# Layer 0's expert table: 80 slots per expert instead of 96

## The reference, cut to what matters

```python
expert = grp[:, None] * EXPERTS_PER_GROUP + local      # two experts per token
counts = jnp.bincount(e_flat, length=N_EXPERTS)
def expert_block(args):
    xb, e = args
    hmid = jax.nn.silu(xb @ e_gate[e]) * (xb @ e_up[e])
    return hmid @ e_down[e]
```

## Time and profile before

| what | value |
|---|---|
| runs | 2742.33, 2744.23, 2746.5 us |
| profiled execution, its own time | 2742.03 us |
| its span | 2740.4 us |
| mean granted TensorE clock | 0.959 of full |
| TensorE busy | 2502.4 us (91%) |
| VectorE busy | 1038.0 us (38%) |
| ScalarE busy | 491.3 us (18%) |
| GpSimd busy | 231.8 us (8%) |
| layer 0's experts in the trace | about 1009 to 1561 us from the span's start |
| layer 1's experts in the trace | about 2215 to 2710 us |

### The profile page before, as it was taken

How to read it: one execution, slowest core, us unless ns; L and a number is a source line. 1 busy time by engine, 2 the same in 40 slices (tenths; PEclk the granted TensorE clock), 3 DMA queues, 4 the chain that set the end, 5 groups by cost and what they waited for, 6 DMA issues and landing times.

```text
span 2740.4 us, 45413 instructions
## 1 busy us (share of the span) xinstructions
PE 2502.4 (91%) x19000; PEld 1530.5 (56%) x19001; DVE 1038.0 (38%) x2398; ACT 491.3 (18%) x978; POOL 231.8 (8%) x391
## 2 busy tenths in 40 slices
PE   7999999999998969999999999999999878888874
PEld 3455545454443457777777655667676544444442
DVE  2226536256465342222222251636457432111112
ACT  2023222222222011111111021323222111101110
POOL 3000001000000001111111110000000011111111
PEclk9989999999999979999999999999999979999997
DMA  9111118242324359999999762123465769999994
GB/s 293 61 62 62 47 43 305 114 142 85 112 87 131 125 193 370 370 374 381 378 383 387 292 203 92 62 77 104 145 185 179 257 265 409 410 418 413 415 404 169
DMA packets 153139, 616.72 MB, mean 225 GB/s; under 512 B 17121, under 2 KB 21489, under 8 KB 136465
## 3 DMA queue, kind: packets, MB, share of 16 engines
q1 hardware_dynamic: 126850, 557.88, 54.4%
q0 software_dynamic: 26192, 57.51, 6.5%
HBM read 598.37 MB, written 46.31 MB: 235 GB/s over the span
## 4 chain that ended last, share of the span: by engine, by line
PE 71%; DMA 15%; DVE 9%; issue 2%; ACT 2%; POOL 0%; DVEq 0%; SPq 0%; POOLq 0%; ACTq 0%
DMA ring<-in_e_down_dram 14%; PE bank L1660 13%; PE bank L1396 12%; PE bank L1288 11%; PE bank L1278 7%; PE score_banks L1677 4%; PE bank L1409 4%; PE score_banks L1697 3%; PE score_banks L1682 2%; PE bank L1567 2%; PE score_banks L1445 2%; PE turned_banks L1455 2%; PE bank L1643 1%; PE bank L1469 1%; PE bank L1317 1%
## 5 line engine op out<-in xcount | busy, mean ns | idle before, releaser
L1660 PEld LDWEIGHTS bank<-scr,ring 128*64 128x64 f32 x8192 | 340.6, 137 | 14.2 <-issue 14.2
L1396 PE MATMUL bank<-HT,ring 128*128 128x512 f32 (+1 forms) x1024 | 347.4, 494 | 0.8 <-ACT scr L1004 0.4
L1660 PE MATMUL bank<-scr,ring 128*64 128x96 f32 x8192 | 346.7, 247 | 1.2 <-DVE scr L2382 1.2
L1288 PE MATMUL bank<-ring,HT 128*128 128x512 f32 (+1 forms) x800 | 303.0, 535 | 0.0
L1653 PE MATMUL bank<-ring,scr 128*64 128x256 f32 x2048 | 239.8, 388 | 44.5 <-DMA ring<-in_e_gate_dram 22.8
L1396 PEld LDWEIGHTS bank<-HT,ring 128*128 128x128 f32 x1024 | 192.1, 192 | 143.2 <-issue 130.9
L1288 PEld LDWEIGHTS bank<-ring,HT 128*128 128x128 f32 x800 | 151.6, 193 | 142.3 <-issue 136.3
L1653 PEld LDWEIGHTS bank<-ring,scr 128*64 128x64 f32 x2048 | 146.5, 139 | 141.4 <-DMA ring<-in_e_gate_dram 41.5
L1278 PE MATMUL bank<-HT,ring 128*128 128x512 f32 (+1 forms) x512 | 196.1, 542 | 1.8 <-ACT HT L1004 1.8
L1697 PE MATMUL score_banks<-ring,scr 128*64 128x512 f32 x512 | 133.7, 670 | 35.5 <-DMA ring<-in_e_down_dram 33.8
L1278 PEld LDWEIGHTS bank<-HT,ring 128*128 128x128 f32 x512 | 97.0, 192 | 91.9 <-issue 88.4
(11 more groups left out here) (267 smaller groups left out, 2715.7 us busy)
## 6 DMA issues: line engine op xcount, KB each, us to landing
ring<-in_e_up_dram SPq DMA_DIRECT2D x64, 2048.0 KB, 22.0
ring<-in_e_down_dram SPq DMA_DIRECT2D x64, 2048.0 KB, 20.9
ring<-in_e_gate_dram SPq DMA_DIRECT2D x64, 2048.0 KB, 21.2
ring<-in_w_in_dram SPq DMA_DIRECT2D x34, 2048.0 KB, 8.0
ring<-in_w_mod_dram SPq DMA_DIRECT2D x32, 1024.0 KB, 5.2
ring<-in_w_mod_dram SPq DMA_DIRECT2D x8, 2048.0 KB, 19.5
ys<-consts POOLq DMA_DIRECT2D x1, 12288.0 KB, 41.7
ring<-in_w_branch_dram SPq DMA_DIRECT2D x4, 2048.0 KB, 7.9
```

What stands on the lines that cost most here:

```text
L1288: m = pe.matmul(bank[:, 0:width], HT[:, k, t * P:t * P + P], w[:, k, 0:width], start=k == 0, stop=k == KT_D - 1)
L1396: m = pe.matmul(bank[:, 0:NQ], w[:, k, (ft % 4) * P:(ft % 4) * P + P], HT[:, k, 0:NQ], start=k == 0, stop=k == KT_D - 1)
L1660: m = pe.matmul(ps[bank][rows_, f * cap:f * cap + cap], w[:, k, f * P + hf * HALF:f * P + hf * HALF + HALF], XTv[:, k, :], start=k == 0, s ...
```

## The change

The table of layer 0 holds 80 slots per expert. The count of column groups stays; the second part of the down product has 16 slots (64 to 79) instead of 32. All that is sized by CAP[0] follows: the transposed tokens, the streamed width in `hidden` (96 to 80), the width of the silu and of the product (384 to 320 elements), the slots of the two indirect DMAs, the blocks of the general path (6 to 7) and the part of `ys` that is cleared early (12288 to 10240 KB). An expert with more than 80 tokens in layer 0 would take the general path, instead of one with more than 96.

```diff
-CAP = (96, 64)
+CAP = (80, 64)
@@ down_held
-                            m = pe.matmul(ps[5][t * 32:t * 32 + 32, 0:256], hv[:, f, HALF:cap], w[:, f, t * 256:t * 256 + 256],
+                            m = pe.matmul(ps[5][t * 32:t * 32 + cap - HALF, 0:256], hv[:, f, HALF:cap], w[:, f, t * 256:t * 256 + 256],
                                           start=f == 0, stop=f == 3)
@@ expert, on VectorE
-                        last = dve.tensor_copy(YS[HALF:cap, j, t * 256:t * 256 + 256], ps[5][t * 32:t * 32 + 32, 0:256])
+                        last = dve.tensor_copy(YS[HALF:cap, j, t * 256:t * 256 + 256], ps[5][t * 32:t * 32 + cap - HALF, 0:256])
```

## The result

The changed kernel took 2714.96 us, median of 4 runs (2712.81 to 2717.82), against 2745.36 us for the kernel before, median of 4 (2742.33 to 2749.89). The ratio is 0.9887, with a 95% interval of 0.9872 to 0.9903. The profiled execution took 2716.85 us, of which the span is 2715.1. Against the profiled execution of before it is 25 us shorter, while the medians are 30 us apart. The profiled execution of before lies 3.4 us under its median, and that of after 1.9 us over.

A forecast was written before the change was run, and what follows sets the result against it. TensorE paces layer 0's experts at 17.22 us, loads close behind at 17.76; layer 1 waits for weights. Loads at 17.0 end the loop 31.2 us sooner, less 1 for clock: 30 off 2742.0 is 2712, median 2714; range 2690 to 2738.

The forecast's parts named there:

- Part 1: Streamed width in the hidden part of layer 0's experts (L1660): 1.7 us less per expert, bounds 0 and 1.8.
- Part 2: Second part of the down product, 16 loaded columns instead of 32: 0 taken, between none and 0.3 us.
- Part 3: Before layer 0's expert loop: slot matmuls 0.5 us and first gate product 1.2 less; first gate load at about 1014.5.
- Part 4: Layer 0's weight loads become late and set the end: 17.0 us per expert, ends 15.95 and 17.76.
- The depth: Weight ring's lead in layer 0, 16.5 us, lasts about 11 experts; the other 19 wait for loads.
- stands whatever TensorE does: Claim that layer 0's loads before the change take 17.73 us per expert independent of TensorE, the DMA queue never being empty.
- The 1 us for the lower clock: Taken off the 31.2 us gain for stretches where TensorE, waiting 1.5 us per expert, falls to the lower clock.
- the unchanged pace: Rival 1: layer 0's loads keep their pace since the tokens don't change; 8.4 us gained, 2736; chance 0.18.
- the loads keep up: Rival 2: layer 0's loads take 15.95 us or less, TensorE sets the end; 2689 to 2692; chance 0.12.
- The uneven dealing: Rival 3: 80-slot indirect DMAs weigh more on the slowest engine; slower above pace 18.04, 2790 at 19.6; chance 0.07.

The follow-up runs named there:

- TensorE's part alone: Against the kernel before: compute loops take 80 slots in layer 0, the table and indirect DMAs keep 96; 2727.33 us, ratio 0.9933.
- the spread order: Changed kernel with layer 0's 80 slots reordered, consecutive tokens 5 partitions apart, filled slots even over 16 groups; 2696.80 us, ratio 0.9822.
- one half of the edit alone: Against the kernel before: table and indirect DMAs have 80 slots in layer 0, compute loops keep 96; 2746.31 us, ratio 1.0002.

## Why the prediction was right

It gave 2714 us, and 2714.96 was measured. Point by point:

- **Part 1**: right. 9.10 us per expert, 1.68 less against the 1.7 taken. The group over 1100 to 1500 has a mean of 233 ns where the earlier trace rows have 246:

```profile
L1660 PE MATMUL bank<-scr,ring 128*64 128x80 f32 x6186 | 220.6, 233 | 0.3 <-DMA ring<-in_e_up_dram 0.3
```

  The width of the stream sets a pair, and not its weight load.
- **Part 2**: right. L1682 takes 1.92 us over 16 loaded columns, 1.93 over 32.
- **Part 3**: the sizes came, the start didn't. The slots' matmuls take 2.32 us and the first hidden part 11.16, against 2.75 and 12.40, 0.43 and 1.24 less:

```profile
999.91 2.32 PE L1630 MATMUL bank<-scr 128*80 128x32 f32 x16
...
1011.04 11.16 PE L1660 MATMUL bank<-scr,ring 128*64 128x80 f32 x256 [1.06 <-DVE scr L2382]
```

  The first part's clock was misread, though: over the 7.3 us the granted clock was 0.77, so that less than half of them were at the half clock, and not most. And the first gate load went out at 1017.97 and not at 1014.5. The stages ahead ended 3 us later in this execution, and over all kernels here that issue lies between 1016.2 and 1020.5. A term of 1.7 us is below that.
- **Part 4**: right in its number and in its kind. Pace 17.07 for 17.0; the last down product follows its weights at once; 5.5 us after them the loop is over. From 1252.92 to 1491.13 the gate loads are issued (1491.13 - 1252.92) / 14 = 17.0 us apart, as the prediction wanted it. The depth lasted for 14 experts and not for 11. The changed kernel's trace has gaps where the landings would be read, but the one with TensorE on 76 slots and the same DMAs has them: its second to fourth gate loads all land after about 11 us (11.2, 10.7, 11.5), and only then do the landings climb, to about 28, where the prediction let them climb from the first. TensorE waits 22.3 us for weights where 25 to 30 were expected, and nearly all of it at e_down and not at all three. I read that as the down load being the latest of the three, so that the stall there gives the next gate and up load the time to land; no run tests it.
- One sentence of the reasoning failed: that the 17.73 us per expert "stands whatever TensorE does". TensorE's part alone brought it to 17.50 with the same 96 slots. That is 7 us of the end. Part of the reason stands in the trace of before: its second to fifth gate loads all land after 9.8 to 10.3 us, so the loads were not behind TensorE from the start.
- That 17.0 came out is in part luck. It was read off a line between 17.76 at 96 slots and layer 1's 15.95 at 64, 0.9 us for each slot per engine. Measured with one TensorE, a slot per engine costs 0.43 (80 to 96) and 0.30 (96 to 112), and the upper end was 17.50. A slope too steep from an end too high met the right number in the middle. On the same line 112 slots would take 18.7, and they took 17.80. Layer 1's end doesn't belong on it either, as the spread order leaves that layer at 15.84.
- The 1 us for the lower clock has no place in the sum. The granted clock did fall to 0.99 on average, and L1677's mean rose from 598 ns to 607, but inside stretches that the loads cover; the last expert ran at the full clock.
- The sum itself was less exact than the medians make it look. It was 2712 for a profiled execution, and 2716.85 was measured: 3.5 us of later start and 2.1 of pace, less the 1 us of clock. The medians agree to 1 us because the two profiled executions lie on opposite sides of theirs, which is luck too.

The rivals: the unchanged pace (2736) fell with 17.07. That the loads keep up (2689 to 2692) fell too, but the spread order, 2696.80, comes to within 5 to 8 us of it. The uneven dealing did not happen with 80 slots, and it is what 76 slots show.

The theory behind the chosen pace, that an indirect DMA is dealt in equal blocks and the first blocks are always full, was tested from three sides. The empty slots count (17.07, 17.50, 17.80 for 80, 96, 112 with the same TensorE). The order counts (17.07 to 16.36 at 80). And a number of slots that doesn't divide well costs more than it saves (17.74 for 76). The three paces agree with 5, 6 and 7 slots per engine, as the rule of the Trainium skill quoted in the prediction has them. An estimate from the rows gives the size too. If an expert's 6.29 MB are shared evenly by 16 engines, each carries 393 KB. The engine with the first block adds 5, 6 or 7 rows of 4 KB gathered and as many scattered, 41, 49 or 57 KB. Divided by the paces that is 25.4, 25.3 and 25.3 GB/s for this engine, one rate for all three; with the slots spread, 2 or 3 rows and 16.36 us give 25.0 to 25.6. It fails in two places: 72 slots, which should be 6 on each of 12 engines, show 17.13 (25.8 GB/s) instead of 17.50, and layer 1 with 4 rows and 15.95 us would need 26.7. Open are these two, what else makes the pace at 96 slots depend on TensorE's, and the small packets at 76.

## What to carry to other kernels

Where two limits stand close together, price each change at both: here one half of the edit alone was worth nothing, the other 18 us, and both together 30. The landing times of prefetched loads show the second limit while it is still hidden; a slope in them, divided by the experts between, gave the second limit's pace ahead of the change to within 0.3 us here (17.76 read, 17.50 measured with the quicker TensorE). Gathers and scatters that share the DMA engines with large loads can hold the load back by the engine that carries most of them. An order that spreads the filled slots was worth 18 us in layer 0, and nothing that could be told in layer 1. Try the number of slots and don't assume it: 80 gained, 76 lost it all in the DMAs, and 72 ran its loop at the pace of 80.

## What was not expected of the hardware

- An indirect DMA of 76 slots instead of 80 makes three times the packets for the same rows (11364 against 3516 in 300 us), and a gather lands in 15.0 instead of 9.3 us.
- The order in which 80 slots are filled, with no byte and no instruction of the loop changed, moved the stage from 393 to 407 GB/s and the kernel by 18 us.
- Empty slots have a price: with the same tokens, 32 more of them cost 26 us (2714.96 to 2741.00).
